# Second half of an output projection between the steps of a stick-breaking attention, in a one-core decoder layer

## What is computed

```python
def stick_breaking_attention(q, k, v):           # 8 heads x 64, tiles of 128 queries
    z = einsum("bhqd,bhkd->bhqk", q_blk, k_pre) * scale
    log_rest = where(strict, log_sigmoid(-z), 0)
    suffix = cumsum(log_rest, reverse=True) - log_rest
    a = where(strict, exp(log_sigmoid(z) + suffix), 0)
    return einsum("bhqk,bhkd->bhqd", a, v_pre)

o_pool = einsum("bsgc,gcd->bsgd", causal_multiscale_pool(u), w_pool) * pool_scale   # 4 groups x 128
x = x + concat([o_sb, o_pool], axis=-1) @ w_out                 # o_sb: 512 wide, o_pool: 512 wide
x = x + memory_cross_attention(rms(x), rms(mem), w_q, w_kv, w_o)
```

## Time and profile before

| | value |
|---|---|
| median of 3 runs | 2017.77 us |
| profiled execution, its span | 2016.6 us |
| PE busy | 1974.8 us (98%) |
| DVE busy | 1328.2 us (66%) |
| ACT busy | 865.4 us (43%) |
| POOL busy | 583.3 us (29%) |
| TensorE clock granted over the span | 0.996 |

### The profile page before, as it was taken

One profiled execution on the slowest core, in us unless ns is written; L12 is line 12 of the kernel. 1 busy time (PEld: TensorE's weight loads), 2 busy tenths in 40 slices (PEclk: granted clock), 3 DMA queues, 4 the chain that ended last, 5 costly groups with the idle time before them and its releaser, 6 DMA issues.

```text
span 2016.6 us, 25198 instructions
## 1 busy us (share of the span) xinstructions
PE 1974.8 (98%) x9369; PEld 1626.8 (81%) x9369; DVE 1328.2 (66%) x1791; ACT 865.4 (43%) x1529; POOL 583.3 (29%) x428
## 2 busy tenths in 40 slices
PE   7999999999999999989999999999999999999998
PEld 6888888887887788766788888888888888878887
DVE  6765565559799732487655555568656556579897
ACT  6534434434445411387634444344443443434444
POOL 1354554530002221065311000221655455410001
PEclk8999999999999999999999999999999999999999
DMA  4223223245500222544134322240322322265102
GB/s 153 78 74 94 84 73 95 84 149 186 187 11 11 68 95 84 148 93 105 42 115 129 113 74 63 63 115 22 105 84 74 94 84 74 73 252 176 63 1 84
DMA packets 217042, 190.15 MB, mean 94 GB/s; under 512 B 7596, under 2 KB 171992, under 8 KB 216920
## 3 DMA queue, kind: packets, MB, share of 16 engines
q1 hardware_dynamic: 216832, 188.51, 30.2%
q10 hardware_dynamic: 88, 0.02, 0.0%
HBM read 152.85 MB, written 35.65 MB: 93 GB/s over the span
## 4 chain that ended last, share of the span: by engine, by line
PE 61%; DVE 4%; ACT 2%; issue 1%; POOL 0%; DVEq 0%; ACTq 0%; POOLq 0%
PE ps L974 19%; PE ps L976 19%; PE ps L975 19%; PE ps L1309 1%; PE ps L1290 1%; DVE rest L2313 1%; PE ps L1276 1%; DVE sr_lo L1895 0%; DVE wb_lo L1895 0%; DVE xn_tmp L1949 0%; PE ps L1280 0%; ACT beta L1781 0%; ACT rest L1762 0%; ACT wb_hi L1461 0%; PE ps L1425 0%
## 5 line engine op out<-in xcount | busy, mean ns | idle before, releaser
L1895 DVE TENSOR_TENSOR w_lo<-st,w_hi 128x512 fp32r<-128x512 f32 x160 | 174.7, 1093 | 177.0 <-ACT w_hi L1461 176.9
L974 PE MATMUL ps<-T_hi,w_lo 128*128 128x512 f32 x640 | 249.7, 390 | 1.2 <-issue 1.1
L975 PE MATMUL ps<-T_lo,w_hi 128*128 128x512 f32 x640 | 249.2, 389 | 0.0
L976 PE MATMUL ps<-T_hi,w_hi 128*128 128x512 f32 x640 | 249.2, 389 | 0.0
L974 PE MATMUL ps<-tr_hi,sr_lo 128*128 128x512 f32 x616 | 242.2, 393 | 3.9 <-DVE tr_lo L1895 3.1
L975 PE MATMUL ps<-tr_lo,sr_hi 128*128 128x512 f32 x616 | 240.1, 390 | 0.0
L976 PE MATMUL ps<-tr_hi,sr_hi 128*128 128x512 f32 x616 | 240.0, 390 | 0.0
L974 PE MATMUL ps<-B_hi,w_lo 128*128 128x512 f32 x576 | 226.4, 393 | 3.5 <-DVE B_lo L1895 2.6
L975 PE MATMUL ps<-B_lo,w_hi 128*128 128x512 f32 x576 | 225.1, 391 | 0.0
L976 PE MATMUL ps<-B_hi,w_hi 128*128 128x512 f32 x576 | 225.1, 391 | 0.0
L974 PE MATMUL ps<-act_hi,wb_lo 128*128 128x512 f32 x384 | 152.4, 397 | 1.7 <-DVE wb_lo L1895 1.6
(11 more groups left out here) (267 smaller groups left out, 4222.8 us busy)
## 6 DMA issues: line engine op xcount, KB each, us to landing
gate_raw<-in_ffn_w_gate SPq DMA_DIRECT2D x44, 512.0 KB, 5.2
up_raw<-in_ffn_w_up SPq DMA_DIRECT2D x44, 512.0 KB, 5.1
h_spill<-up_s SPq DMA_DIRECT2D x66, 256.0 KB, 2.0
piece_A<-in_ffn_w_down SPq DMA_DIRECT2D x32, 512.0 KB, 4.5
piece_B<-h_spill SPq DMA_DIRECT2D x32, 512.0 KB, 6.0
wa_raw<-in_w_in SPq DMA_DIRECT2D x16, 512.0 KB, 4.0
wb_raw<-in_w_out SPq DMA_DIRECT2D x16, 512.0 KB, 3.8
wb_raw<-in_mem_w_kv SPq DMA_DIRECT2D x16, 512.0 KB, 3.8
```

Of the source, the lines that this page charges most:

```text
L974: pe.matmul(to, w_lo, m_hi, start=first, stop=False, skip_group_check=joins)
L975: pe.matmul(to, w_hi, m_lo, start=False, stop=False, skip_group_check=joins)
L976: return pe.matmul(to, w_hi, m_hi, start=False, stop=last, skip_group_check=joins)
L1895: return dve.tensor_tensor(to, value, plain(hi), ALU.subtract)
```

## The change

- **Pooled half moved.** The pooled half gets buffers of its own (`pl_hi`, `pl_lo`), and so do the attention's outputs (`o_hi`, `o_lo`). Its part of the projection becomes FILLS = 16 units (8 output tiles x 2 token halves) of 4 chunks x 3 matmuls, issued by `fill` from step 5 on: 1, 1 and 2 chunks in three steps, so to step 52. They use PSUM bank FILL_BANK, the former STILL_BANK. DVE adds each unit to `xT` in the step of its last chunk, and the next unit waits for that add (`f_add`).
- **Its weights.** 8 loads of 256 KB on SP's queue between the stack loads of the heads, one copy on ACT and one subtraction on DVE for each (`fw_hi`, `fw_lo`).
- **Scan operand.** The scan's second operand is an element of `ones`, in SBUF, no longer one of PSUM.
- **Values in one piece.** `values(w)` makes the products of four tiles in one step, not in two pieces.
- **Output projection after the steps.** `out0` and `out1` have 4 steps each, each making two output tiles of 4 chunks from one 512 KB load (24 matmuls as before). The first makes 3 chunks of both tiles, waits for the last outputs, then the fourth chunks.
- **Order.** `out0` 0 and 1, memT, `out0` 2 and 3; then mk, mk, out1, mv, mv, xn, xn. The squares of the memory rows and their Newton chain (`mem_rms`) move into the last steps of the loop.
- A few semaphores are merged.

```diff
+        FILLS = 2 * DC
+        FILL_FROM, FILL_CHUNKS = TURN_LAG + 1, (0, 1, 2, 4)
+        FILL_STEPS = len(FILL_CHUNKS) - 1
...
-        B_STEPS = tiles("out0", 0, 1) + [("mem_rms",)] + tiles("out0", 1, 3) + [("memT",)] + tiles("out0", 3, DC)
+        B_STEPS = tiles("out0", 0, 2) + [("memT",)] + tiles("out0", 2, QC)
         for j in range(0, DC, 2):
             B_STEPS += tiles("mk", j, j + 2) + [("tot", 4)] * (j == 0)
-            B_STEPS += tiles("out1", j, j + 1) + [("bc", 4)] * (j == 0)
-            B_STEPS += tiles("mv", j, j + 2) + xn_steps(4, j, j + 1)
-            B_STEPS += tiles("out1", j + 1, j + 2) + xn_steps(4, j + 1, j + 2)
+            B_STEPS += tiles("out1", j // 2, j // 2 + 1) + [("bc", 4)] * (j == 0)
+            B_STEPS += tiles("mv", j, j + 2) + xn_steps(4, j, j + 2)
...
+            fill_load(0)
             for h in range(2, HEADS):
                 stack_load(h)
+                for j in {3: (1, 2, 3), 5: (4, 5), 7: (6, 7)}.get(h, ()):
+                    fill_load(j)
...
+            def fill(n):
+                u, c = divmod(n, QC)
+                j, half = divmod(u, 2)
+                if c == 0:
+                    if half == 0:
+                        pe.wait_ge(s_mw_lo, j + 2)
+                    if u:
+                        pe.wait_ge(f_add, u)
+                mm = three(ps[:, FILL_BANK, :], fw_hi[:, j % 2, c, :], fw_lo[:, j % 2, c, :],
+                           pl_hi[:, c, tok(half)], pl_lo[:, c, tok(half)], c == 0, c == QC - 1)
+                if c == QC - 1:
+                    mm.then_inc(f_out, 1)
...
+                for n in fills_at(s):
+                    fill(n)
                 if 0 <= s - TURN_LAG < M:
                     turn(s - TURN_LAG)
                 if s == M + 4:
-                    pe.wait_ge(s_scan, M)
+                    pe.wait_ge(f_add, FILLS)
                     tile(B_STEPS[0])
-                if VALUE_LAG <= s < M + VALUE_LAG and (s - VALUE_LAG) % 4 < 2:
-                    values(*divmod(s - VALUE_LAG, 4))
+                if VALUE_LAG <= s < M + VALUE_LAG and (s - VALUE_LAG) % 4 == 0:
+                    values((s - VALUE_LAG) // 4)
...
-                dve.tensor_tensor_scan(r[:, ::-1], r[:, ::-1], ps[:, STILL_BANK, 0:1].broadcast_to([P, n]), 1.0,
+                dve.tensor_tensor_scan(r[:, ::-1], r[:, ::-1], ones[:, 0:1].broadcast_to([P, n]), 1.0,
                                        ALU.mult, ALU.bypass).then_inc(s_scan, 1)
...
+                unit = fill_done(s)
+                if unit is not None:
+                    j, half = divmod(unit, 2)
+                    dve.wait_ge(f_out, unit + 1)
+                    dve.tensor_tensor(xT[:, j, tok(half)], ps[:, FILL_BANK, :], xT[:, j, tok(half)],
+                                      ALU.add).then_inc(f_add, 1)
+                j = fill_weight_at(s - 1)
+                if j is not None:
+                    dve.wait_ge(s_mw_hi, j + 2)
+                    lo(fw_lo[:, j % 2], fw_raw[:], fw_hi[:, j % 2]).then_inc(s_mw_lo, 1)
```

More of the change, by code:

```diff
@@ L573, in layer_program, with tiles_made @@
         ADDS = ("out0", "out1", "o0", "o1")
+        PAIRED = ("out0", "out1")
+        def tiles_made(step):
+            return 2 if step[1] in PAIRED else 1
         b_first, b_hi_of, n_units, n_hi = {}, {}, 0, 0
@@ L578, in layer_program @@
             made = {"PV": HD, "tile": 1}.get(step[0], 0)
+            if step[0] == "tile":
+                made = tiles_made(step)
             if step[:2] == ("tile", "mv"):
@@ L613, in layer_program @@
         assert all(end <= 4 for _, end in z_bank)
-        STILL_BANK = a_bank[A_PROJ + 4]
-        TURN_BANKS = [b for b in (4, 5, 6) if b != STILL_BANK]
-        assert STILL_BANK != 7
+        FILL_BANK = a_bank[A_PROJ + 4]
+        TURN_BANKS = [b for b in (4, 5, 6) if b != FILL_BANK]
+        assert FILL_BANK != 7
         def turns(m):
@@ L1248, in _ @@
                         mm.then_inc(a_half, 1)
-            pe.wait_ge(s_wp, 1)
+            pe.wait_ge(s_mw_lo, 1)
             def pool_map(k):
@@ L1339, in tile, with stick_part @@
                     return
+                if kind in PAIRED:
+                    half = int(kind[-1])
+                    def stick_part(i, d):
+                        cols_ = slice(i * P, (i + 1) * P)
+                        return three(ps[:, 4 + (k + i) % 4, :], wide(wb_hi, n % 2)[:, d, cols_],
+                                     wide(wb_lo, n % 2)[:, d, cols_], o_hi[:, d, tok(half)], o_lo[:, d, tok(half)],
+                                     d == 0, d == QC - 1)
+                    if n == 0:
+                        for i in range(2):
+                            if i:
+                                pe.wait_ge(s_aT, copied(M - 1, False))
+                                pe.wait_ge(s_aT_dve, copied(M - 1, True))
+                            for d in range(QC - 1):
+                                stick_part(i, d)
+                        pe.wait_ge(s_o_free, W - 1)
+                        for i in range(2):
+                            stick_part(i, QC - 1).then_inc(b_out, 1)
+                        return
+                    for i in range(2):
+                        if n == 1 and i:
+                            pe.wait_ge(s_o_free, W)
+                        if k + i >= 4:
+                            pe.wait_ge(b_free, k + i - 3)
+                        for d in range(QC):
+                            mm = stick_part(i, d)
+                        mm.then_inc(b_out, 1)
+                    return
                 if k >= 4:
@@ L1342, in tile @@
                 bank = ps[:, 4 + k % 4, :]
[L1344 to L1348, removed]
+                for d in range(DC):
+                    ends = d == 0, d == DC - 1
                     if kind == "o1" and j == 0 and d == HD * (MHEADS - 1):
@@ L1812, in _ @@
                         b_weight(b_tile[step] + 2)
-                    if kind in ADDS:
-                        act.wait_ge(b_free, k + 1)
[L1815 to L1824, removed]
+                    if kind in PAIRED:
+                        for i in range(2):
+                            act.wait_ge(b_free, k + i + 1)
+                            square(4 + int(kind[-1]), 2 * j + i)
+                    elif kind in ADDS:
+                        act.wait_ge(b_free, k + 1)
+                        square(6 + int(kind[-1]), j)
                 elif step[0] == "memT":
@@ L2352, in _ @@
                     _, kind, j = step
-                    if kind in ADDS:
+                    if kind in PAIRED:
+                        half = int(kind[-1])
+                        if k == 0:
+                            dve.wait_ge(f_add, FILLS)
+                        for i in range(2):
+                            dve.wait_ge(b_out, k + i + 1)
+                            dve.tensor_tensor(xT[:, 2 * j + i, tok(half)], ps[:, 4 + (k + i) % 4, :],
+                                              xT[:, 2 * j + i, tok(half)], ALU.add).then_inc(b_free, 1)
+                    elif kind in ADDS:
                         half = int(kind[-1])
@@ L2371, in _ @@
                         b_weight(b_tile[step] + 2)
[L2372 to L2380, removed]
                 elif step[0] == "memT":
```

119 lines of the change are left out of this document (84 added, 35 removed).

## The result

| | before | after |
|---|---|---|
| median of the runs beside each other (4 and 4) | 2018.41 us | 2031.16 us (2030.28 to 2031.27) |
| ratio to before, 95% interval | 1 | 1.0062 [1.0048, 1.0076] |
| profiled span | 2016.6 us | 2029.5 us |
| last transpose of `beta` (end of the steps) | 985.9 | 1034.4 |
| from there to the end of the span | 1030.7 | 995.1 |

What follows compares the result with a forecast made beforehand. PE was taken as the bound, busy for 98% of the span, with waits going round a ring in the steps. Stage +58, moved products -43.5 and stalls +5 gave +20 on 2016.6, median 2037 us; range 2012 to 2052.

Steps and rivals of the forecast that it cites:

- The sign and its cause: Whole kernel: slower (0.71), because the scan with SBUF operand and POOL's multiplication exclude each other.
- rival 2: Stick-breaking steps: exclusion holds but hides under PE, 44 us a pair, 38 in the last; 2018 us, chance 0.15.
- Stage: Stick-breaking steps: three pairs of 49 us and one of 42, 189 against 131, so +58 us.
- The larger of both, group by group: Filled head pair: the larger of PE's and DVE's work in each group, summed to 48.7 us, taken as 49.
- rival 1: Steps: SBUF scan costs nothing, PE sets the pace, 43.3 us a pair, last 32.7; 2011 us, chance 0.18.
- Moved products: Projection stage after the steps: 192 products leave it, making it 43.5 us shorter.
- Stalls behind the steps: Projection after the steps: PE waits for late wb_lo where xn steps stand together, +5 us (0 to 9).
- PE's wait for the add: Filled steps: a unit's first fill waits for DVE's add of the unit before; 53 us a pair if held on top.
- rival 3: Steps: exclusion and PE's new wait add, 53 us a pair and 44 in the last; 2051 us, chance 0.14.
- Loads: SP's queue in the steps: 8 weight loads among the stack loads cost nothing, unless a stack load comes late.
- faster: Whole kernel: beats the one before, by rival 1 without its slow edge and rival 2's low edge; chance 0.17.
- the floor: Steps and projection: without any PE idle the stage grows by 28 us against 43.5 saved, net -15.5 us.

Runs made afterwards that it cites:

- the dense run: Changed kernel with xn ahead of out1 and PSUM scans in unfilled steps, plus two fill chunks every step from 5 to 36: 2027.30 us, ratio 1.0042.

## Why the prediction was right, and where its sizes were off

**The sign and its cause: right.** The operand alone costs 19 us on the kernel before, and without a partner to exclude, the changed kernel comes level with it.

**How it acts in the filled pairs: wrong in part.** Of the marks named, multiplications of 1023 columns at 2.5 to 3.7 us came in six of eight. Scans of 1024 columns took 3.9 and 4.0 us in two of eight (2.7 in a third), and 2.26 to 2.28 in the second and third pair. The pairs of 46 us came, but not with DVE near full: in the second, DVE is busy for 35.8 of 46.3 us and PE for 44.3. So in a filled pair PE sets the pace, as rival 2 had it, and the exclusion adds 1.5 to 2.2 us.

**The time: 2037 forecast, 2031.2 measured.** In spans, +20 was forecast and +12.9 came. It is partly luck that they lie so close: the stage was put 9.5 us too long and the stalls 2.9 too short. The range of 2012 to 2052 holds rival 2's time too, so the time alone does not tell the two apart. The 1.2 us from span to median was small as well: for the changed kernel it is 1.7 (2031.16 and 2029.5). The three terms:

- *Stage, +58 forecast, +48.5 measured.* The step that failed is "The larger of both, group by group: 9.1 + 15.8 + 10.8 + 13 = 48.7". The filled pairs took 46.3 and 45.5, not 49; the last took 39.8 and was 9.1 longer than before, as forecast (+9.3). The large group was to be held by DVE for 15.8 us and took 12.4 in the second pair (14.1 and 13.7 in the first and third); the groups around it took 10.2, 11.3 and 12.4 where 9.1, 10.8 and 13 were forecast. The rings do carry work from the large group into its neighbours, and the run that moved the fills between the groups leaves the pair's sum as it is. A filled pair is PE's work of 41.9, some 2.2 of starts and latencies (44.1 without exclusion, where rival 1 had 43.3), and 1.5 to 2.2 of exclusion. That is about the middle between the forecast's 49 and rival 2's 44.
- *Moved products, -43.5: right.* With the xn chunks elsewhere the rest is 43.0 shorter.
- *Stalls behind the steps, +5 forecast, 7.9 measured* (43.5 - 35.6). 2.0 of these are the clock: PE runs at half clock for 3.4 us at 1128.4. The run with PSUM scans in the unfilled steps has the same instructions there and full clock, and its rest is 993.1, 37.6 shorter than before. So the stalls themselves are 5.9. The place was right: PE waits 1.3, 1.7 and 1.8 us for `wb_lo` before out1 tiles, where it waited 0.5 three times. In all it waits 6.2 us for `wb_lo`, before 1.6. Three of these waits, of 0.4 us each and in other places, are for a subtraction whose stretching the forecast had not seen: it falls beside POOL's sum of squares and takes 2.02 us, not 1.23, the exclusion again. DVE and POOL in time:

```profile
1098.05 2.02 DVE L1996 TENSOR_TENSOR wb_lo<-wb_raw,wb_hi 128x1024 fp32r<-128x1024 f32 x1 [1.65 <-ACT wb_hi L1551]
...
1095.73 3.25 POOL L968 TENSOR_TENSOR ssq<-ssq,sq 128x512 f32<-128x512 f32 x2 [17.61 <-ACT sq L1559]
```

**Small terms.** Values in one piece at nothing: right. PE's wait for the add is 1.8 us in a pair, and rival 3's 53 a pair did not come. Loads at nothing: right here, but with a thin margin, as the dense run shows.

**The rivals.** Rival 1's condition, no exclusion, was made true in one run: it gives 2018.4, not 2011. It put the stage at +32 and the stalls at 5; in the profiled execution, of a span of 2014.0, they are +35.0 and 5.9. The filled pairs grew by 8.8, 11.4 and 11.3 where it had 10.6 each, and the last by 3.5 where it had nothing (fills run in its first steps). The median lies 2.6 us above that execution. So "faster" was worth less than the 0.17 given to it: even with its one condition the change would have been level. Rival 2's time, 2018, was that of a version with a mended order and PSUM scans in the unfilled steps, not of this one.

**Why the change cannot win much.** Of the 43.5 us of products moved into the steps, the filled steps give back most: without exclusion the stage is still 35.0 us longer (1020.9 against 985.9). So the steps had 8.5 us of free PE time for these products, not the 15.5 of the floor. The stalls behind the steps take 5.9 of it in the same execution, and the median of that version is level with the kernel before.

## What to carry to other kernels

Before giving away an "idle" PSUM bank, ask who reads it: an operand that is only a placeholder may be what keeps DVE off two SBUF reads, and with POOL at work beside it that was 19 us here. When work moves from a full stage into one with gaps, not all of the gaps take it (8.5 of 15.5 us here), and what it had covered where it was lies bare: here that was worth 5 to 6 us, and a reordering got it back. Where rings carry several tiles, sum each engine over a whole round before taking the larger, and don't take the larger tile group by tile group.

## What the hardware showed that was not expected

PE's granted clock fell to half (from 2.4 to 1.2 GHz) for stretches of 3.4 to 10.2 us. The kernel before has none in the steps, nor have the two runs with the short multiplication. The changed one has them at 869.0 (3.4 us), 1008.9 (6.8) and 1029.4 (3.4, behind the last scan), and one at 1128.4, 94 us behind the steps; the kernel before with the SBUF operand has five, 23.9 us in all. The mean granted clock was 0.89 in the 47 us shown of the changed kernel's last pair and 0.77 in the 15 us shown of the other. It is not the exclusion as such that brings the clock down: the kernel before with the operand in the score banks has no exclusion, and yet 3.4 and 10.2 us at half clock in its first pair. Ahead of the fall at 1008.9 PE stood idle for 1.98 us and waited for a copy of `aT`:

```profile
1007.72 1.06 PE L1340 MATMUL ps<-ident,beta 128*128 128x128 f32 x8 [1.98 <-ACT aT L1551]
```

With the SBUF operand alone PE is idle for 2.32 us just ahead of each of the four falls in the pairs; the longest idle of PE in the steps of the kernel before is 1.3 us. But the changed kernel also has an idle of 1.92 us at 965 with no fall behind it, where the same steps in the run with the xn chunks moved have one.

What such a stretch costs can be read where the same instructions ran at either clock. Where PE sets the pace, 3.4 us at half clock cost 1.6 in the third pair (47.1 with the xn chunks moved, 45.5 without) and 2.0 behind the steps (995.1 and 993.1). In the last pair, where DVE and POOL mostly set it, the third group takes 9.5 us with 6.8 at half clock and 8.8 with 3.4, so 0.7 for 3.4 us. By these, an estimate: of the 5.6 us that the last pair lost, 1.4 are the clock and about 4 the exclusion itself. In the kernel before with the SBUF operand the four groups of the largest tiles, which ran at full clock but for their last 0.8 us at most, are 2.7 to 3.3 us longer each, 11.4 in all; the most that the clock can have added to its 19 us lies in the groups behind them, which lost 9.0, and in 3.4 us at half clock behind the last scan.
